# Index scores of a sparse attention: two of eight heads rectified and weighted by VectorE straight from PSUM, half sums added by GpSimd, dense products issued in couples

## The reference, cut to what matters

```python
dots = jnp.einsum('bthd,bsd->bths', qi.astype(jnp.float32), k_idx.astype(jnp.float32))
score = jnp.einsum('bths,bth->bts', jax.nn.relu(dots), wi.astype(jnp.float32))
causal = key_pos[None, :] <= t_pos[:, None]
score = jnp.where(causal[None], score, -jnp.inf)
_, idx = lax.top_k(score, top_k)
```

## Time and profile before

| what | us |
|---|---|
| median of 3 runs | 2229.24 |
| lowest and highest run | 2227.84 and 2229.49 |
| span of the profiled execution | 2227.9 |
| TensorE busy in the span | 2197.6 (99%) |
| VectorE busy | 1055.1 (47%) |
| ScalarE busy | 801.4 (36%) |
| GpSimd busy | 931.6 (42%) |

### The profile page before, as it was taken

How to read it: one execution, slowest core, us unless ns; L and a number is a source line. 1 busy time by engine, 2 the same in 40 slices (tenths; PEclk the granted TensorE clock), 3 DMA queues, 4 the chain that set the end, 5 groups by cost and what they waited for, 6 DMA issues and landing times.

```text
span 2227.9 us, 30109 instructions
## 1 busy us (share of the span) xinstructions
PE 2197.6 (99%) x12142; PEld 1781.3 (80%) x12142; DVE 1055.1 (47%) x1503; ACT 801.4 (36%) x832; POOL 931.6 (42%) x513
## 2 busy tenths in 40 slices
PE   8999999999999999999999999999999999999998
PEld 6888888776767888888888888888888878888887
DVE  5433202655864253332046441647566546888701
ACT  4222313537745342222143542433334244222222
POOL 4555444443332445555445244423233343444343
PEclk9999999999999999999999999999999999999999
DMA  4222323343232333322233123313121243333223
GB/s 155 95 94 94 95 95 113 81 77 55 64 119 95 104 95 96 101 95 94 94 105 94 58 75 96 95 39 96 58 77 57 88 149 104 95 94 94 68 94 112
DMA packets 162444, 203.93 MB, mean 92 GB/s; under 512 B 12260, under 2 KB 117031, under 8 KB 162343
## 3 DMA queue, kind: packets, MB, share of 16 engines
q1 hardware_dynamic: 155584, 197.69, 29.4%
q10 hardware_dynamic: 6759, 4.80, 0.7%
HBM read 191.97 MB, written 10.49 MB: 91 GB/s over the span
## 4 chain that ended last, share of the span: by engine, by line
PE 94%; DVE 2%; ACT 2%; issue 1%; POOL 0%; DMA 0%; SPq 0%; POOLq 0%; ACTq 0%; DVEq 0%
PE PS L212 24%; PE PS L214 23%; PE PS L213 23%; PE PS L243 2%; PE PS L245 2%; PE PS L244 2%; PE PS L2523 2%; PE PS L2525 2%; PE PS L2524 2%; PE PS L1159 1%; PE PS L2175 1%; PE PS L1692 1%; PE PS L2192 1%; PE PS L1075 1%; POOL wl L203 0%
## 5 line engine op out<-in xcount | busy, mean ns | idle before, releaser
L203 POOL TENSOR_TENSOR wl<-raw,wh 128x1024 fp32r<-128x1024 f32 x335 | 855.4, 2568 | 1193.2 <-ACT wh L192 1193.2
L212 PE MATMUL PS<-h_hi,wh 128*128 128x512 f32 x1696 | 677.5, 399 | 4.7 <-ACT stage_a L857 2.3
L214 PE MATMUL PS<-h_hi,wl 128*128 128x512 f32 x1696 | 661.7, 390 | 0.0
L213 PE MATMUL PS<-h_lo,wh 128*128 128x512 f32 x1696 | 661.2, 390 | 0.0
L192 ACT ACTIVATE wh<-raw 128x2048 fp32r<-128x2048 f32 (+1 forms) x214 | 332.7, 1555 | 826.6 <-PE PS L214 709.2
L212 PEld LDWEIGHTS PS<-h_hi,wh 128*128 128x128 f32 x1696 | 318.8, 188 | 89.2 <-issue 18.1
L214 PEld LDWEIGHTS PS<-h_hi,wl 128*128 128x128 f32 x1696 | 318.6, 188 | 67.3
L213 PEld LDWEIGHTS PS<-h_lo,wh 128*128 128x128 f32 x1696 | 319.1, 188 | 61.7 <-issue 1.0
L689 DVE SCALAR_TENSOR_TENSOR xT<-PS,xT 128x512 f32<-128x512 f32 x32 | 21.9, 689 | 283.8 <-PE PS L214 283.8
L572 DVE TENSOR_TENSOR act_lo<-work,act_hi 128x1024 f32 (+1 forms) x33 | 64.3, 1950 | 179.6 <-ACT act_hi L519 179.6
L212 PE MATMUL PS<-act_hi,wh 128*128 (+1 forms) x352 | 137.2, 390 | 0.0
(11 more groups left out here) (453 smaller groups left out, 3056.2 us busy)
## 6 DMA issues: line engine op xcount, KB each, us to landing
raw<-in_w_in_dram SPq DMA_DIRECT2D x94, 512.0 KB, 4.6
raw<-in_w_up_dram SPq DMA_DIRECT2D x82, 512.0 KB, 4.7
raw<-in_w_down_dram SPq DMA_DIRECT2D x132, 256.0 KB, 2.8
raw<-in_w_gate_dram SPq DMA_DIRECT2D x42, 512.0 KB, 3.9
raw<-in_w_in_dram SPq DMA_DIRECT2D x20, 256.0 KB, 3.6
raw<-in_w_out_dram SPq DMA_DIRECT2D x16, 256.0 KB, 2.8
raw<-in_w_ret_br_dram SPq DMA_DIRECT2D x8, 512.0 KB, 4.1
gates<-stage SPq DMA_DIRECT2D x16, 256.0 KB, 5.6
```

What stands on the lines that cost most here:

```text
L203: ins = nc.gpsimd.tensor_tensor(wl[:, slot, part], raw[:, slot, part], wh[:, slot, part].bitcast(F32), ALU.subtract)
L212: nc.tensor.matmul(dst, sh, mh, start=start, stop=False)
L213: nc.tensor.matmul(dst, sh, ml, start=False, stop=False)
L214: return nc.tensor.matmul(dst, sl, mh, start=False, stop=stop)
```

## The change

Heads 0 and 4 of each block (`straight(n)`) no longer go through ScalarE. VectorE reads their dot from PSUM, takes the maximum with zero and multiplies by the weight in one TENSOR_SCALAR with two operations. Heads 1 to 3 are added to head 0 in `score` as before, heads 5 to 7 to head 4 in a second tile, `score2`, which lies in `work`. GpSimd adds `score2` to `score` before it sets the keys ahead. Relu steps are counted anew (`relus`), 18 where there were 24. A new semaphore, `a_straight`, counts VectorE's six straight steps, and dot n waits for it where dot n-3 was a straight one. The eight dense products stand as four couples, behind n = 7, 11, 15 and 19.

```diff
         for i in range(1, NT):
-            pool.wait_ge(a_rused, 8 * i)
+            pool.wait_ge(a_rused, 6 * i)
+            pool.wait_ge(a_straight, 2 * i)
+            s = score[:, soff[i]:soff[i + 1]]
+            pool_link(pool.tensor_tensor(s, s, score2[:, soff[i]:soff[i + 1]], ALU.add))
             d = score[:, soff[i] + i * P:soff[i + 1]]
...
+    STRAIGHT = (0, 4)
+    score2 = work[:, 2 * SPAN:2 * SPAN + soff[4]]
+
+    def straight(n):
+
+        return n % 8 in STRAIGHT
...
                 if n >= 3:
-                    pe.wait_ge(a_relu, n - 2)
+                    if straight(n - 3):
+                        pe.wait_ge(a_straight, straights(n - 2))
+                    else:
+                        pe.wait_ge(a_relu, relus(n - 2))
...
-                if n % 2 and 5 <= n <= 19:
-                    fill(pe, 1)
+                if n % 4 == 3 and 7 <= n <= 19:
+                    fill(pe, 2)
...
-                act.wait_ge(a_dot, n + 1)
-                if n >= 2:
-                    act.wait_ge(a_rused, n - 1)
-                act.activation(lgi[:, n % 2, 0:(i + 1) * P], PS[:, dot_bank(n), 0:(i + 1) * P], ACT.Relu).then_inc(a_relu, 1)
+                if not straight(n):
+                    m = relus(n)
+                    act.wait_ge(a_dot, n + 1)
+                    if m >= 2:
+                        act.wait_ge(a_rused, m - 1)
+                    act.activation(lgi[:, m % 2, 0:(i + 1) * P], PS[:, dot_bank(n), 0:(i + 1) * P], ACT.Relu).then_inc(a_relu, 1)
...
-                dve.wait_ge(a_relu, n + 1)
                 w = widx[:, i, h:h + 1]
-                if h == 0:
-                    ins = dve.tensor_scalar(s, lgi[:, n % 2, 0:(i + 1) * P], w, None, ALU.mult)
+                if straight(n):
+                    dve.wait_ge(a_dot, n + 1)
+                    dve.tensor_scalar(s if h == 0 else s2, PS[:, dot_bank(n), 0:(i + 1) * P], 0.0, w, ALU.max,
+                                      ALU.mult).then_inc(a_straight, 1)
                 else:
-                    dve.wait_ge(a_rused, n)
-                    ins = dve.scalar_tensor_tensor(s, lgi[:, n % 2, 0:(i + 1) * P], w, s, ALU.mult, ALU.add)
-                ins.then_inc(a_rused, 1)
+                    m = relus(n)
+                    half = s if h < 4 else s2
+                    dve.wait_ge(a_relu, m + 1)
+                    dve.wait_ge(a_rused, m)
+                    dve.wait_ge(a_straight, straights(n))
+                    dve.scalar_tensor_tensor(half, lgi[:, m % 2, 0:(i + 1) * P], w, half, ALU.mult, ALU.add).then_inc(a_rused, 1)
```

More of the change, by code:

```diff
@@ L753, in two_blocks_kernel @@
     fl_mm, fl_ev = sem("fl_mm"), sem("fl_ev")
+    a_straight = sem("a_straight")
     qb_set = sem("qb_scaled")
@@ L1065, in dot_bank, with straights, relus @@
         return 4 + n % 3
+    STRAIGHT = (0, 4)
+    score2 = work[:, 2 * SPAN:2 * SPAN + soff[4]]
+    def straight(n):
+        return n % 8 in STRAIGHT
+    def straights(n):
+        return sum(straight(m) for m in range(n))
+    def relus(n):
+        return n - straights(n)
     def index_pe(pe):
@@ L1101, in index_dve @@
         for i in range(1, NT):
-            s = score[:, soff[i]:soff[i + 1]]
+            s, s2 = score[:, soff[i]:soff[i + 1]], score2[:, soff[i]:soff[i + 1]]
             for h in range(8):
-                dve.wait_ge(a_relu, n + 1)
                 w = widx[:, i, h:h + 1]
-                if h == 0:
-                    ins = dve.tensor_scalar(s, lgi[:, n % 2, 0:(i + 1) * P], w, None, ALU.mult)
-                else:
-                    dve.wait_ge(a_rused, n)
-                    ins = dve.scalar_tensor_tensor(s, lgi[:, n % 2, 0:(i + 1) * P], w, s, ALU.mult, ALU.add)
-                ins.then_inc(a_rused, 1)
+                if straight(n):
+                    dve.wait_ge(a_dot, n + 1)
+                    dve.tensor_scalar(s if h == 0 else s2, PS[:, dot_bank(n), 0:(i + 1) * P], 0.0, w, ALU.max,
+                                      ALU.mult).then_inc(a_straight, 1)
+                else:
+                    m = relus(n)
[4 more added lines that the diff above has]
+                    dve.scalar_tensor_tensor(half, lgi[:, m % 2, 0:(i + 1) * P], w, half, ALU.mult, ALU.add).then_inc(a_rused, 1)
                 n += 1
@@ L1141, in stick_pe @@
         fill(pe, AHEAD)
-        pe.wait_ge(a_relu, 8 * (NT - 1))
+        pe.wait_ge(a_relu, 6 * (NT - 1))
+        pe.wait_ge(a_straight, 2 * (NT - 1))
         pe.wait_ge(*by_act("vb"))
```

## The result

The changed kernel takes 2231.56 us in the median of 21 runs, the kernel before 2229.24 in as many beside it. The ratio is 1.0012, with a 95% interval of 1.0006 to 1.0017: about 2.3 us, slower beyond the interval, and within the 0.2% that the forecast calls the same. The forecast was 2232.1.

The account below looks back on a forecast made before the run. TensorE was taken to bound the kernel, busy 2197.6 of 2227.9 us. The terms 0.74 + 1.22 + 0.72 + 0.19 gave +2.9 us, put on the median 2229.24 for 2232.1; range 2229.0 to 2234.3.

Parts of the forecast that it names:

- The mechanism: Index stage: with products in couples, every fourth dot waits for VectorE's straight step, 0.5 to 0.8 us each; chance 0.74.
- The stage: Index stage, from the first dot to the four products: forecast 21.7 us long where it was 18.86.
- the sum: Added time of all dots in the index stage: 0.74 + 1.22 + 0.72 + 0.19 = +2.9 us.
- The fours of 384 and 512 columns: Dots n = 8 to 23: +0.61 for each four of 384 columns; at 512, +0.72 with products, +0.19 without.
- the nearest row: Price of the straight step, from a profiled TENSOR_SCALAR reading 512 columns of PSUM, 743 ns: 0.74, narrower 0.61 and 0.48.
- the first block: Dots n = 0 to 7, 256 columns: dot 7 waits for VectorE's queue, 5.87 us where it was 5.13, +0.74.
- the release: From a reader's end to the TensorE instruction it frees: 0.14 from VectorE, 0.05 from ScalarE, taken as 0.10 us.
- GpSimd's additions: Adding score2 to score in each block: 0.72, 0.99 and 1.26 us, forecast to cost TensorE nothing.
- The low half: GpSimd's low half of the next weights, behind the third addition: ends near 520.7, TensorE asks at 522.05, 1.3 to spare.
- The second addition: GpSimd's addition in the second block: forecast to clear VectorE's next weighted sum by about 1.2 us.
- ScalarE's lost relus: Six fewer relus on ScalarE, two of which took 0.66 to 1.09 us together: buys nothing in mid-stage.
- the span of the profiled execution: Whole kernel before: 2227.9 us, 1.3 below the runs' median and said to agree with the lowest run.

Follow-up runs that it names:

- e2: The kernel before with its eight products as four couples and nothing else changed, all heads through ScalarE: 2230.71 us against 2228.3, ratio 1.0009.
- e1: The changed kernel with its eight products one at a time again, straight heads and GpSimd additions kept: 2228.67 us, kernel before 2228.3, ratio 1.0.
- e3: The changed kernel with a fourth bank for the dots from n = 8 on: 2227.69 us against 2228.3 for the kernel before, ratio 0.9998.
- e5: The changed kernel with a fourth bank from n = 8, single products in the first block, earlier copy of gate job 0: 2226.24 us against 2229.36, ratio 0.9986.
- e6: The kernel before, without straight heads or GpSimd addition, given e5's banks, products and gate copy: 2227.74 us against 2229.36, ratio 0.9993.
- e4: The changed kernel with one more GpSimd TENSOR_TENSOR of 2048 columns behind block 1's select, as a probe: one run of 2231.31 us.

## Why the prediction was right

**The mechanism held.** Dot n waits for the reader of dot n-3, and a couple uncovers that wait. The weight loads show it in the changed kernel, e2 brings it with no straight head at all, e1 removes it with all straight heads left in, and the fourth bank removes it with the couples left in place.

**The sizes.** The stage grew by 2.51 us; the sum was 2.87. The fours of 384 and 512 columns came within 0.05 of the forecast, because a straight step from PSUM cost what the nearest row said. The term that was mis-sized is the first block: +0.53 in place of +0.74. Its chain was priced link by link, and several links were a little long: the straight step started 0.73 us behind the first dot rather than 0.79, the three sums and head 4 ended at 3.39 rather than 3.56 behind it (494.74 + 0.48 - 491.83), and the release took 0.05, not 0.10. The last of these was the 0.14 of the earlier trace rows, which I had averaged in.

**What was hidden.** GpSimd's additions cost 0.73, 0.99 and 1.29 us (forecast 0.72, 0.99, 1.26) and nobody waits for them. The low half had 1.25 us to spare (forecast 1.3). The second addition missed VectorE's next weighted sum by 0.89 us, where the forecast had about 1.2. In e1, e3 and e5 the two overlap: GpSimd's select behind that addition then lasts 0.55 to 0.66 us and not 0.29, and nobody waits for it. ScalarE's lost relus bought nothing in the changed kernel, as forecast.

**The total agrees partly by chance.** The span after is 2230.8, the very number of the sum, but 0.70 us of its growth lies ahead of the index stage, in code that the change doesn't touch, and a net 0.35 was given back far behind it: 0.70 + 2.51 + 0.04 - 0.35 = 2.9. The medians differ by 2.32, which the stage's 2.51 explains within the interval. That the stage's end reaches the total is borne out by the runs: in e1, e2, e3, e5 and e6 the medians moved by +0.37, +2.41, -0.61, -3.12 and -1.62 us, where the stages moved by +0.16, +1.77, -0.26, -2.33 and -1.74.

**One step of the argument was wrong without harm.** The prediction, like the section on the time before, says that the span of the profiled execution agrees with the lowest run. For the kernels run here the profiled execution's time is known beside its span: 2232.47 for 2230.8, 2229.35 for 2227.6, 2224.92 for 2223.2. It is 1.7 us above the span, so the 2227.9 of before belongs to a run near 2229.6, close to the median. That the shift was put on the median was right; the reason given for it was not.

## What to carry to other kernels

Filler work between two dependent steps of a ring of buffers is not an interruption but the cover of the reader: before bundling it to save a switch (here 0.2 us each), add up the time from producer through reader to release, and compare it with what is left in between. If the bundle is wanted, pay for it with one more buffer: four couples cost 1.77 us with three banks (e2), and three couples with a fourth bank, single products in the first block and an earlier gate copy gave a stage 1.74 us shorter without straight heads (e6) and 2.33 us shorter with them (e5). Taking work off an engine that nobody waits for gains nothing: in the fours with products, ScalarE's lost relus changed no piece (e1 against before).

## What the runs showed of the hardware that wasn't expected

Pairs of dots in an unbroken row are faster than pairs that stand alone: eight records of 384 columns span 1.49 us from the first to the next product (495.48 to 496.97 in e5), where two separate pairs took 2 x 0.85. The fours with four banks were 0.2 us shorter than I had worked out for that reason.

Some 110 us behind the change, in the sparse stage, the granted clock falls in some executions and not in others: in before, after, e1, e2 and e6, but not in e3, e4 and e5. TensorE waits there 1.3 us for VectorE in each of them. The timeline of the changed kernel has that wait and the next one:

```profile
628.31 0.33 PE L1294 MATMUL PS<-ident,pr 128*128 128x128 f32 x1 [1.29 <-DVE pr L1335]
...
632.89 0.50 PE L212 MATMUL PS<-h_hi,wh 128*128 128x512 f32 x1 [0.47 <-ACT stage_a L858]
```

The same two rows of e3's timeline:

```profile
624.25 0.33 PE L1299 MATMUL PS<-ident,pr 128*128 128x128 f32 x1 [1.30 <-DVE pr L1340]
...
627.41 0.50 PE L212 MATMUL PS<-h_hi,wh 128*128 128x512 f32 x1 [0.58 <-ACT stage_a L858]
```

The same work takes 4.58 us in the one and 3.16 in the other. The view by windows (length, busy us of TensorE, its loads, VectorE, ScalarE, GpSimd, then the clock) shows the lower of the two levels, 0.50 or 1.2 GHz, in the changed kernel:

```profile
629.00:631.00 2.00, 2.00 (x8) 1.48 (x7) 1.55 (x11) 0.67 (x4) 0.00 (x0) 0.50 0.18 67
```

In e3 it shows full clock throughout the sparse stage's first 20 us:

```profile
615.00:635.00 20.00, 17.72 (x96) 11.54 (x93) 14.20 (x55) 8.29 (x24) 6.67 (x3) 1.00 0.65 176
```

The wait ahead of it is as long in both, so it isn't that wait alone which decides. What does wasn't tried. It puts 1.4 us into a single span or not, which is more than half of what the change costs. Before and after both have it, 4.43 and 4.58 us for the stretch, so it adds little to their difference; but part of e5's shorter span is this and not the stage.
